# The branches of four latent blocks in one stage, and rows at four places of the recurrence

## What is computed

```python
h = rmsnorm(x, norm_mix) * (1 + sc1) + sh1
qkv, z, bf, bb, af, ab, u, vg, ga, gb = split_last(h @ w_in, ...)
o = o_f + flip(o_b)                      # gated delta recurrence over q, k, v, in both directions
o = rmsnorm(o, dn_norm) * silu(z)        # 8 heads of 128
u = gelu(u)
vg = rmsnorm(gelu(vg), gm_norm)
gm = u * (einsum('gts,bnsgc->bntgc', gm_w_s, vg) + gm_b_s)
merged = sigmoid(ga) * (o @ w_branch_a) + sigmoid(gb) * (gm @ w_branch_b)
x = x + gt1 * (merged @ w_out)
h2 = rmsnorm(x, norm_ffn) * (1 + sc2) + sh2
s = (h2 @ w_query) . sub_keys            # per head two score lists of 128 keys
sv, si = top_k(s, 16)                    # best 16 of each list
best, pos = top_k(sv[0][:, None] + sv[1][None, :], 16)     # best 16 of 256 sums
x = x + gt2 * sum over 8 heads and 16 picks of gelu(h2 . peer_u[e]) * softmax(best) * peer_v[e]
y = rmsnorm(x, norm_final)
```

## Time and profile before

| | us |
|---|---|
| median of 3 runs | 5606.19 (5598.96 to 5611.48) |
| the profiled execution, its own time | 5607.62 |
| its span | 5605.8 |
| PE busy | 3073.4 (55%) |
| DVE busy | 3904.2 (70%) |
| POOL busy | 2940.7 (52%) |
| ACT busy | 519.0 (9%) |

### The profile page before, as it was taken

One profiled execution on the slowest core, in us unless ns is written; L12 is line 12 of the kernel. 1 busy time (PEld: TensorE's weight loads), 2 busy tenths in 40 slices (PEclk: granted clock), 3 DMA queues, 4 the chain that ended last, 5 costly groups with the idle time before them and its releaser, 6 DMA issues. The chain is left out here.

```text
span 5605.8 us, 41938 instructions
## 1 busy us (share of the span) xinstructions
PE 3073.4 (55%) x16118; PEld 2149.6 (38%) x16118; DVE 3904.2 (70%) x4330; ACT 519.0 (9%) x857; POOL 2940.7 (52%) x1532
## 2 busy tenths in 40 slices
PE   5989988998997886898998967000000000000000
PEld 2787955448996875455554444000000000000000
DVE  1340027976664436665776679899999999999998
ACT  1521002422221000000000000000000000000000
POOL 0131003745552210544543520888888888888887
PEclk7999989999999998999999988555555555555555
DMA  9819878973227996897999851999999999999998
GB/s 388 345 56 344 320 300 321 395 316 110 80 76 302 391 388 239 336 358 310 420 420 404 358 225 61 422 420 422 422 419 421 419 421 420 420 408 422 422 422 363
DMA packets 272942, 1892.52 MB, mean 338 GB/s; under 512 B 31780, under 2 KB 36132, under 8 KB 49511
## 3 DMA queue, kind: packets, MB, share of 16 engines
q0 software_dynamic: 194560, 1409.51, 61.5%
q1 hardware_dynamic: 71558, 440.26, 20.1%
q10 hardware_dynamic: 6624, 40.07, 1.8%
HBM read 1870.78 MB, written 18.94 MB: 337 GB/s over the span
## 5 line engine op out<-in xcount | busy, mean ns | idle before, releaser
L216 PE MATMUL ps<-arena_sb 128*128 128x128 f32 (+2 forms) x9216 | 1889.4, 367 | 128.4 <-PEq L1634 32.6
L316 POOL DMA_INDIRECT arena_sb<-peer_v,arena_sb x640 | 1303.6, 2037 | 840.5 <-DVE arena_sb L368 426.0
L368 DVE SCALAR_TENSOR_TENSOR arena_sb<-arena_sb 128x2048 f32<-128x2048 f32 x635 | 1497.8, 2359 | 193.7 <-DMA arena_sb<-peer_v,arena_sb 120.6
L216 PEld LDWEIGHTS ps<-arena_sb 128*128 128x128 f32 x9216 | 1328.9, 196 | 706.8 <-issue 324.4
L363 DVE CUSTOM_DVE_ANT_0 arena_sb<-arena_sb 128x2048 f32<-128x2048 f32 x640 | 1475.3, 2319 | 176.6 <-DMA arena_sb<-peer_u,arena_sb 176.3
L316 POOL DMA_INDIRECT arena_sb<-peer_u,arena_sb x640 | 1258.8, 1967 | 459.2 <-DVE arena_sb L363 266.9
L262 POOL DMA_DIRECT2D arena_sb<-w_mod x64 | 34.8, 544 | 617.3 <-PE ps L223 485.9
L838 POOL TENSOR_TENSOR arena_sb<-arena_sb 128x1024 f32<-128x1024 f32 x60 | 185.1, 3095 | 217.3 <-ACT arena_sb L1098 165.0
L1500 PE MATMUL ps<-arena_sb 128*128 128x512 f32 x640 | 279.4, 599 | 30.7 <-PEq L1354 30.0
L1419 DVE TENSOR_TENSOR arena_sb<-ps,arena_sb 128x128 f32<-128x128 f32 (+1 forms) x96 | 35.2, 378 | 350.4 <-PE ps L216 350.1
L908 PE MATMUL ps<-arena_sb 128*128 128x64 f32 x1760 | 206.4, 275 | 0.0
(11 more groups left out here) (222 smaller groups left out, 2299.9 us busy)
## 6 DMA issues: line engine op xcount, KB each, us to landing
arena_sb<-w_mod POOLq DMA_DIRECT2D x64, 1024.0 KB, 8.2
arena_sb<-w_qkv SPq DMA_DIRECT2D x48, 1024.0 KB
arena_sb<-w_ga SPq DMA_DIRECT2D x48, 1024.0 KB
arena_sb<-w_gb SPq DMA_DIRECT2D x48, 1024.0 KB
arena_sb<-w_out SPq DMA_DIRECT2D x48, 1024.0 KB
arena_sb<-w_query SPq DMA_DIRECT2D x48, 1024.0 KB
arena_sb<-w_mod SPq DMA_DIRECT2D x32, 1024.0 KB
arena_sb<-w_z SPq DMA_DIRECT2D x24, 1024.0 KB
```

Source lines behind the costliest of these rows:

```text
L216: mm = pe.matmul(out, weights[:, k * P:(k + 1) * P], x[:, k, :], start=(k == 0), stop=(k == chunks - 1))
L316: nc.gpsimd.indirect_dma_start(slot, None, a["peer_v" if adds else "peer_u"], bass.IndirectOffsetOnAxis(ap=g.index[:, p:p + 1], axis=0)).t ...
L368: nc.vector.scalar_tensor_tensor(out=total, in0=rows, scalar=g.weight[:, p:p + 1], in1=total, op0=ALU.mult, op1=ALU.add).then_inc(t.rows_u ...
```

## The change

- **One branch stage.** `branches` runs for context and for latent; lead and rest start with `merge`. `g.on` and `g.gm` of lead and rest are slices of latent's arrays, which stay in place until rest's merge; lead's other buffers (`merged`, `x`, `h2`, ...) move elsewhere. The rows behind the stage are [4] for each of the 8 z tiles, 34 behind vg and [4] behind each of 7 u tiles: 94 (before: 24 in lead's branches, 76 in rest's). Four gathers are issued at the start, and GpSimd stages head n+1 ahead of the gathers behind head n.
- **Recurrence.** The four rows of a batch stand behind levels 1, 2, 3 and 5.
- **Output projection of rest.** 32 rows in place of 38, none behind the last four banks; the context's final norm stands behind the second quarter, on VectorE and ScalarE.
- **Scores.** The sums are 4 x 16 + 12 x 4 = 112 per block in place of 256 (a pair of ranks i, j counting from 0 can only be among the best 16 if (i+1)(j+1) is at most 16); positions are turned back into ranks by a few more operations. Rest has ten rows ahead of the heads, as before, and ten more between them.
- In all 449 row steps stand ahead of `experts`, 451 before.

```diff
+FULL = 4
+FEW = 4
+PAIRS = FULL * 16 + (16 - FULL) * FEW
...
-                    if n < loads and k in (2, 3):
-                        use_rows(dve, nc, t, behind[n][k - 2:k - 1])
-                if n < loads:
-                    use_rows(dve, nc, t, behind[n][2:4])
+                    if n < loads and k in (1, 2, 3, 5):
+                        use_rows(dve, nc, t, behind[n][k * 3 // 4:k * 3 // 4 + 1])
...
-    behind = take(t, [0] * (2 * H + 1) if ctx else [1] * H + [9] + [1] * (H - 1) + [0] if nb == 1 else
-                  [4, 3] * (H // 2) + [27] + [3] * (H - 1) + [0], 4)
+    behind = take(t, [0] * (2 * H + 1) if ctx else [4] * H + [34] + [4] * (H - 1) + [0], 4)
...
+            if not ctx:
+                gather_rows(pool, nc, t, a, [range(t.held, t.held)], 0)
             pool.wait_ge(o_step, 2 * nb + 2)
             for n in range(H):
                 after(pool, oT_ps, n - 1)
...
-                else:
-                    gather_rows(pool, nc, t, a, behind, n)
+                elif n:
+                    gather_rows(pool, nc, t, a, behind, n - 1)
...
-    behind = take(t, [4, 3] * 5 + [3, 0] if last else [0] * (4 * nb), 4)
+    behind = take(t, [4, 4, 4, 4, 4, 4, 3, 3, 2, 0, 0, 0] if last else [0] * (4 * nb), 4)
...
+                if last and c == 1:
+                    finish_context()
                 if c == 2:
...
-    behind = take(t, [0 if ctx else 10 if nb == 3 else 4], 4 if nb == 3 else 3)
+    behind = take(t, [10, 2, 1, 2, 1, 2, 1, 1, 0] if nb == 3 else [0 if ctx else 4] + [0] * H, 4 if nb == 3 else 3)
...
-                step.step(nc.vector.tensor_tensor(
-                    sums.rearrange("p b (i j) -> p b i j", i=TOPK),
-                    value[0].unsqueeze(3).to_broadcast([P, nb, TOPK, TOPK]),
-                    value[1].unsqueeze(2).to_broadcast([P, nb, TOPK, TOPK]), ALU.add))
+                for lo, hi, w, o in ((0, FULL, TOPK, 0), (FULL, TOPK, FEW, FULL * TOPK)):
+                    n = hi - lo
+                    ins = nc.vector.tensor_tensor(
+                        sums[:, :, o:o + n * w].rearrange("p b (i j) -> p b i j", i=n),
+                        value[0][:, :, lo:hi].unsqueeze(3).to_broadcast([P, nb, n, w]),
+                        value[1][:, :, 0:w].unsqueeze(2).to_broadcast([P, nb, n, w]), ALU.add)
+                step.step(ins)
...
+            if g in (context, latent):
+                branches(nc, t, a, g)
+                retire()
             if g is not latent:
-                for stage in (branches, merge, output_projection, expert_input, scores):
+                for stage in (merge, output_projection, expert_input, scores):
```

More of the change, by code:

```diff
@@ L1147, in _ @@
         def _(sp):
[L1148 removed]
+            for n in range(H):
                 load_tile(sp, t, a["w_z"], n, n)
@@ L1690, in _ @@
                 nc.scalar.activation(query[n % 2], t.ps[:, n % 4, 0:nt], ACT.Copy).then_inc(query_done, 1)
+                if n % 2 and n > 4:
+                    gelu_rows(act, nc, t, behind[n // 2 - 1])
+            for rows in behind[H - 1:]:
+                gelu_rows(act, nc, t, rows)
             if ctx:
@@ new lines, in route @@
+                for out, w in ((down[0], TOPK), (down[1], FEW)):
+                    ins = nc.vector.scalar_tensor_tensor(out=out, in0=first, scalar=-float(w), in1=at, op0=ALU.mult,
+                                                         op1=ALU.add)
+                step.step(ins)
+                step.step(nc.vector.scalar_tensor_tensor(out=second, in0=down[1], scalar=float(FULL * FEW - FULL * TOPK),
+                                                         in1=down[0], op0=ALU.add, op1=ALU.max))
```

103 lines of the change are left out of this document (55 added, 48 removed).

## The result

| | before | after |
|---|---|---|
| median of the runs, us | 5607.51 (4 runs, 5598.96 to 5611.48) | 5513.17 (4 runs, 5506.77 to 5521.08) |
| profiled execution, us (its span) | 5607.62 (5605.8) | 5512.66 (5510.9) |
| ratio of the runs, 95% interval | | 0.9834 (0.9817 to 0.9852) |

The profiled execution is 95.0 us shorter; the prediction had 86.2. First the table of stretches of the changed kernel, one row per stage, as in the earlier trace rows: length, busy time and instructions of PE, PEld, DVE, ACT and POOL, granted clock, DMA share, GB/s.

The account below looks back on a forecast made before the run. DMA was taken to bound the expert rows and one-block branches, TensorE the three-block branches, dependent steps the recurrence, VectorE the three-block scores. Terms summed to -86.2 us from 5607.6, giving 5521, range 5497 to 5563.

Parts of the forecast that it names:

- Branch stages, -65.2: Branch stages: two stages of 136.0 and 310.2 us become one four-block stage of 381.0 us, saving 65.2.
- The scaling by 4/3: Joint branch stage: TensorE's steady three-block pace times 4/3 gives 113.6, 110.0 and 136.6 us, together 360.2.
- 8.9 us are barrier and semaphore clearing: Branch stage's tail: 8.9 us from the end of VectorE's last product to the merge were taken as barrier and semaphore clearing.
- Why the holes go: Branch stage: staging head n+1 ahead of the gathers ends transposes' waits for GpSimd, 14.07 us steps where 10.65 is possible.
- Rival (a): Joint branch stage: DMA holds it at 338 GB/s, 416 us in place of 381, total 5556; chance 0.11.
- Recurrence, -18.2: Latent recurrence: moving two rows ahead of level 6's end saves 2.6 us in each of 7 batches, 18.2 in all.
- 3.2 freed, 0.6 paid at level 5: Recurrence, per batch: 3.2 us come free behind level 6; the row behind level 5 starts the last multiplications 0.6 later.
- Rival (b): Recurrence gives nothing: the row behind level 1 slows GpSimd's mask products and their chain becomes the wait; 5539, chance 0.09.
- Output projection, -15.0: Three-block output projection: fewer rows, none behind the last quarter, and a later final norm free the last bank, saving 15.0 us.
- Rival (d): Output projection: rows behind the second quarter still fill the third, so it saves only 5, total 5531; chance 0.07.
- Routing, +9.1: Three-block scores: shorter scans and sums save about 15 us, ten rows between heads cost 24.2, net +9.1.
- Rival (c): Joint stage: TensorE runs at its lower clock, 1.2 GHz; slower, 5880 if wholly there; chance 0.03.

Follow-up runs that it names:

- Experiment 10: Changed kernel without the three gathers ahead at the joint stage's end; the lead block's merge gathers those rows itself: 5515.7 us.
- Experiment 6: Changed kernel with GpSimd's order in the branch stage as before, all gathers behind a head ahead of staging the next head: 5523.0 us.
- experiment 1: Changed kernel with the recurrence's rows placed as before, behind levels 2 and 3 and two behind level 6: 5542.5 us.
- experiments 1 and 2: Changed kernel with the recurrence's rows as before, 5542.5 us; and with one row behind level 6, none behind level 5, 5525.7 us.
- experiment 3: Changed kernel with next staging and masks of levels 3 and 4 ahead of GpSimd's wait for the state at the turn: 5511.0 us.
- experiments 5 and 9: Changed kernel with the context's output written ahead of the last two tile loads, 5514.9 us; and with gathers ahead before the last quarter's adds, 5511.1 us.
- experiment 8: Changed kernel with the last output projection as before, 38 rows in place of 32 and the context's final norm at its start: 5515.7 us.
- experiment 7: Changed kernel with the three-block group's routing over all 256 sums a head, as before: 5536.0 us.
- experiment 11: Changed kernel with masks ahead of the turn's wait, output write and gathers ahead moved earlier, joint-stage rows 5, 5, 5, 5, 4, 4, 0: 5480.3 us.

## Why the prediction was right, and where not

The time (5521 against 5513, within the range) and the side were right, and the four rivals did not happen. The structure of the sum held, but that the total came this close is in part luck: the tail of the joint stage and the turn of the direction cost some 13 us that I did not have, TensorE's clock in the recurrence gave back as much, and 11.9 us of the measured 94.8 are the two rows that are scatter, or mostly so. Part by part:

- **Branch stages, -65.2; measured -60.1.** The scaling by 4/3 held: tiles of 14.17 and 17.06 us against 14.2 and 17.1, w_vg 110.0 against 110.0, 365.0 us to the last mixing against 364.5. The step that failed is the tail: "8.9 us are barrier and semaphore clearing". Experiment 10 shows 0.3 for the barrier; the 8.9 hung on the rows gathered ahead (5.2 until their last packet, and 3.7 behind it). The later these go out, the later the stage ends, and the change has four rows where there were three, so the last gather is issued at 2068.86, after VectorE's last product, where before it had gone at 2541.32, before it. The tail took 21.0 in place of 16.5.
- **"Why the holes go"** was a wrong cause for a right number, which is luck. Experiment 6: the new order of GpSimd saves 2.5 us; the longer tile does the rest.
- **Rival (a), DMA at 338 GB/s.** The w_vg part ran at 394 GB/s and unbroken. The 123 us that go with the figure of the Trainium skill (DMA: Bandwidth & Descriptors, Where 436 GB/s comes from) did not come. The figure there is half of what a stack of memory gives, one core's share of two; only one core works here, and its 394 and 419 GB/s are not bound by that share.
- **Recurrence, -18.2; measured -22.1**, and the row move by itself 22.9 (experiment 1); periods of 50.7 where I had said 52.7. "3.2 freed, 0.6 paid at level 5" was 3.0 and nothing: the level-5 and level-6 adds are 5.4 us apart with and without the row. Two things were missed and partly cancel: TensorE's lower clock, 1.5 us in five of the seven periods and 2.8 in two, some 13 us in all, which hung on the same idle time (experiments 1 and 2), and 8.9 us at the turn of the direction, shown by experiment 3. The trace of before had both: the idle time of 3.74 before the transposes, and GpSimd's order, in which the masks stand behind the wait for a load. **Rival (b)** fell: with rows behind levels 1, 2 and 3 a mask product takes 4.26 us in each, and the levels still step in 5.52.
- **Output projection, -15.0; measured -12.1.** The last bank waits for TensorE and is read 15.3 us earlier, so the mechanism was right; what was mis-sized is the end, 17.5 us in place of 14.3, where I subtracted the backlog and took the rest as fixed. The context's output, which stands in SyncE's queue behind tiles that wait for TensorE, had landed before the last bank was read (3246.94, against 3248.92); now it is issued together with the last bank's read and shares DMA with the gathers (experiments 5 and 9). And the term says less than it seems: it is six rows moved, and they come back as 15.8 us of expert rows (experiment 8). In my sum this was hidden in the balance of two rows. **Rival (d)** did not occur.
- **Routing, +9.1; measured +9.0**, its shorter scans 14.1 against 14.6 (experiment 7). The net of my own terms, 24.2 less 14.6, is +9.6, not +9.1: a slip of 0.5. **Expert rows, +5.1; measured +3.7**, 828 gathers at 2.53.
- **Rival (c)**, the clock, decided nothing: 0.96 over the joint stage. Its first tile and its last mixings ran partly at the lower level, at some 5 us.

Left open: why the opening stage scatters by 9 us and the lead merge by 9, and what passes in the 2 to 5 us between the last packet of the gathers and the next stage, was not tried.

## What to carry to other kernels

Look at the end of a stage for what is in flight, not for what works: the barrier behind GpSimd's gathers waited until they had landed (14.9 us here, of which the barrier was 0.3), while SyncE's tile loads did not hold it up. So such gathers go out ahead of the last work, and a write that the program waits for does not stand in a queue behind loads that wait for a slot. When work is packed around a chain of dependent steps, look for the one irregular round, here the turn of the direction: slack that hid a load of 8 us there goes first. And count a moved row twice, where it leaves and where it arrives; a stage that gets shorter by giving work away has gained nothing yet.

## What the hardware showed that I had not expected

- TensorE's clock enters a recurrence through gaps of a few microseconds: after 3.74 us of idle time eight transposes took 1.79 and 1.97 us in the two batches shown, at the lower level of the clock for most of the stretch, after 1.77 and after 0.51 us 1.09 at 1.00. Two rows of VectorE cost 3.0 us directly and 1.5, in some batches 2.8, in this way.
- A barrier behind the last instruction took 0.3 us with nothing in flight, and 14.9 with three gathered rows of 1 MB on their way: 10.3 until their last packet, and 4.7 behind it. A tile load of SyncE that was still moving 1.9 us into the next stage did not hold it (experiment 11).
- Where VectorE's row and a GpSimd product meet, the one that starts second is delayed. In the changed kernel's recurrence all 18 rows that started ahead of a product took 2.28 us, as alone, and the product up to 4.26 in place of 2.35; rows that started while one ran took 2.94 and 3.81 us at the turn, and 4.28 in the first batch.
